# A hybrid decoder layer on one core: k's token rows turned in 32 by 32 blocks by VectorE instead of by TensorE, and a new order of the work before the first FFN products

## What is computed

```
def _mixer_inputs(x, shift, scale, g_pre, w_in, b_f):
    h = _rmsnorm(x, g_pre) * (1.0 + scale) + shift
    q, k, v, f, u, bg, cg, ga, gb = _split_cols(h @ w_in, IN_SIZES)
    logf = jax.nn.log_sigmoid((f + b_f).astype(jnp.float32))
    heads = lambda t: t.reshape(B, T, N_HEADS, HEAD_DIM)
    return heads(q), heads(k), heads(v), logf, cg * u, bg, ga, gb
...
def _finish(x, o, y_conv, bg, ga, gb, gate1, shift2, scale2, gate2, ...):
    m = (jax.nn.sigmoid(ga) * a + jax.nn.sigmoid(gb) * b) @ w_o
    x = x + gate1 * _rmsnorm(m, g_post1)
    h = _rmsnorm(x, g_pre2) * (1.0 + scale2) + shift2
    g, u = jnp.split(h @ w_ffn_in, 2, axis=-1)
    f = (jax.nn.silu(g) * u) @ w_ffn_out
    return x + gate2 * _rmsnorm(f, g_post2)
```

## Time and profile before

| | |
|---|---|
| time, median of 3 runs | 1783.26 us (1783.14 to 1783.98) |
| the profiled execution's own time | 1783.0 us |
| its span | 1781.4 us |
| PE busy | 1768.5 us (99% of the span) |
| DVE busy | 911.0 us (51%) |
| ACT busy | 693.8 us (39%) |
| POOL busy | 26.1 us (1%) |
| data moved | 382.38 MB, 215 GB/s on average |
| granted PE clock | 1.0 of full speed |

### The profile page before, as it was taken

The page is one execution under the profiler, slowest core; times in us unless marked ns, Lnnn a source line. Parts: engine busy times, 40 slices in busy tenths (PEclk is TensorE's granted clock), DMA queues, the critical chain, the costliest instruction groups (busy, mean ns, idle before and its releaser), DMA issues.

```text
span 1781.4 us, 31779 instructions
## 1 busy us (share of the span) xinstructions
PE 1768.5 (99%) x13592; PEld 1664.2 (93%) x13592; DVE 911.0 (51%) x1137; ACT 693.8 (39%) x809; POOL 26.1 (1%) x76
## 2 busy tenths in 40 slices
PE   8999999999999999999999999999999999999999
PEld 6888888897699999998979999999999999999998
DVE  4666663245644344455686444434443445566565
ACT  5332232235643333343354233333333334445454
POOL 0000100001000000000000000000000000000000
PEclk9999999999999999999999999999999999999999
DMA  9988578856754444458866444444444444444441
GB/s 380 409 333 336 214 309 343 355 200 223 262 185 165 163 159 167 162 196 343 332 245 265 142 166 165 165 165 165 165 165 165 165 163 166 164 163 164 163 161 71
DMA packets 59234, 382.38 MB, mean 215 GB/s; under 512 B 6912, under 2 KB 7728, under 8 KB 17026
## 3 DMA queue, kind: packets, MB, share of 16 engines
q1 hardware_dynamic: 57632, 378.27, 56.0%
q0 software_dynamic: 1328, 2.58, 0.4%
q10 hardware_dynamic: 178, 0.13, 0.0%
HBM read 376.15 MB, written 4.81 MB: 214 GB/s over the span
## 4 chain that ended last, share of the span: by engine, by line
PE 96%; DMA 1%; DVE 1%; ACT 1%; issue 1%; SPq 0%; DVEq 0%; ACTq 0%
PE bank L675 29%; PE bank L677 29%; PE bank L676 28%; PE bank L695 3%; PE bank L685 1%; PE bank L972 1%; DMA ada<-in_w_ada 1%; PE bank L1102 1%; PE bank L1071 0%; PE bank L1290 0%; DMA ada_o<-in_w_ada 0%; PE bank L1041 0%; PE bank L951 0%; PE bank L1051 0%; PE bank L898 0%
## 5 line engine op out<-in xcount | busy, mean ns | idle before, releaser
L675 PE MATMUL bank<-a_lo,w_hi 128*128 128x288 f32 x3624 | 1077.0, 297 | 1.4 <-DVE a_lo L1978 0.7
L676 PE MATMUL bank<-a_hi,w_hi 128*128 128x288 f32 x3624 | 1069.1, 295 | 0.0
L677 PE MATMUL bank<-a_hi,w_lo 128*128 128x288 f32 x3624 | 1065.5, 294 | 0.0
L1794 DVE TENSOR_TENSOR w_lo<-raw,w_hi 128x2048 fp32r<-128x2048 f32 x239 | 547.9, 2292 | 699.9 <-ACT w_hi L1327 699.2
L1327 ACT CAST w_hi<-raw 128x2048 fp32r<-128x2048 f32 x238 | 453.9, 1907 | 850.2 <-PE bank L677 824.7
L675 PEld LDWEIGHTS bank<-a_lo,w_hi 128*128 128x128 f32 x3624 | 678.9, 187 | 20.7 <-issue 19.2
L677 PEld LDWEIGHTS bank<-a_hi,w_lo 128*128 128x128 f32 x3624 | 682.6, 188 | 0.0
L676 PEld LDWEIGHTS bank<-a_hi,w_hi 128*128 128x128 f32 x3624 | 680.3, 188 | 0.0
L1906 DVE TENSOR_TENSOR a_lo<-hid,a_hi 128x1152 fp32r<-128x1152 f32 x44 | 59.4, 1351 | 12.3 <-ACT a_hi L1351 12.3
L1351 ACT CAST a_hi<-hid 128x1152 fp32r<-128x1152 f32 x44 | 50.7, 1154 | 0.0
L675 PE MATMUL bank<-o_lo,w_hi 128*128 128x288 f32 x128 | 37.9, 296 | 0.0
(11 more groups left out here) (387 smaller groups left out, 973.4 us busy)
## 6 DMA issues: line engine op xcount, KB each, us to landing
raw<-in_w_ffn_in SPq DMA_DIRECT2D x88, 1024.0 KB, 4.8
raw<-in_w_in SPq DMA_DIRECT2D x75, 1024.0 KB, 7.9
ada<-in_w_ada SPq DMA_DIRECT2D x60, 1024.0 KB, 8.9
raw<-in_w_ffn_out SPq DMA_DIRECT2D x44, 1024.0 KB, 4.8
ada_o<-in_w_ada SPq DMA_DIRECT2D x24, 1024.0 KB, 8.4
raw<-in_w_o SPq DMA_DIRECT2D x16, 1024.0 KB, 4.9
ada<-in_w_ada SPq DMA_DIRECT2D x16, 512.0 KB, 12.6
raw<-in_cache_k SPq DMA_DIRECT2D x16, 512.0 KB, 4.2
```

The costliest lines, as they stand in the source:

```text
L675: pe.matmul(acc, w_hi[buf][:, a, cols], lo[:, kt, :], start=first and a == 0, stop=False)
L676: pe.matmul(acc, w_hi[buf][:, a, cols], hi[:, kt, :], start=False, stop=False)
L677: mm = pe.matmul(acc, w_lo[buf][:, a, cols], hi[:, kt, :], start=False, stop=last and a == tiles - 1)
L1794: tt(w_lo[buf][:, :, :], raw[s][:, :, :], w_hi[buf][:, :, :].bitcast(F32), ALU.subtract).then_inc(raw_turn, 1)
```

## The change

It has two parts that do not touch each other.

1. k is no longer turned by PE. DVE transposes each half of kT in blocks of 32 by 32 (`turn_k_blocks`, one instruction on 128 partitions by 1152 numbers for each half) into a new buffer `k_blocks`. In it a token's channels lie on the partition of the token in pieces of 32, so ACT issues the stores piece by piece (`store_k`): for each half 16 stores for the prompt (32 partitions, 8 blocks, runs of 32 numbers, which is 128 bytes; 32 KB each) and 4 for the samples (16 KB each), 40 in all. The six `turn_rows` and six `copy_row` of k are gone, and so are POOL's two stores of k.
2. Around the first FFN product: the last squares are added on PE by one more matmul and no longer by DVE; the samples of the last w_o tiles are evicted first; two w_ada slots move to another region, so that their loads wait for an earlier product; the w_ada slots are used in another order, 8 of them before the first FFN product, 3 between its halves and 1 inside the second half; and a_hi and a_lo of tiles 0 and 1 are made and waited for one by one (`h2_tiles`).

The core of the diff:

```diff
-    ROWS = ([("k", half, b) for half in range(2) for b in range(3)]
-            + [("v", 0, 0), ("v", 0, 1), ("v", 1, 0), ("v", 1, 1), ("v", 0, 2), ("v", 1, 2)])
+    ROWS = ([("v", 0, 0), ("v", 0, 1), ("v", 1, 0), ("v", 1, 1), ("v", 0, 2), ("v", 1, 2)])
+    K_STORES = 4 * (KA + 2)
...
@@ SP, load_f1 @@
+                    if first and t == 3:
+                        sp.wait_ge(mm_turn, MT * (SPLIT + N_F1 - 2))
+                        for q in range(2, SK):
+                            load_t(q)
                     load_w(N_F1 + PER_F1 * i + t, t % RAW, slot(w_ffn_in, part * F1S + i, k))
                     if first and t == 3:
-                        sp.wait_ge(mm_turn, MT * (SPLIT + N_F1))
-                        for q in range(2, SK):
-                            load_t(q)
-                        for q in range(SK):
-                            sp.wait_ge(ada_turn, RAW + SK * ADA_T + q + 1)
+                        for q, used in enumerate((1, 2, 5, 6)):
+                            sp.wait_ge(ada_turn, RAW + SK * ADA_T + used)
                             sp.dma_start(ada_o[q][:, :, :], slot(w_ada, ADA_T + 2 - SPARE, q)).then_inc(ada_full[q], 16)
...
@@ PE @@
                 if u == 19:
                     sums_of_lf()
-                    pe.wait_ge(ada_turned, 1 + len(ADA_AT))
-                    pe.wait_ge(ada_mods, A_B1 + 1)
-                    pe.wait_ge(bank_turn, BT + MT * (G_QKV + 3))
-                    turn_rows(0)
-                    turn_rows(1)
                 if u == 20:
                     turn_suf()
-                if u == 21:
-                    pe.wait_ge(sufT_done, 1)
-                    pe.wait_ge(bank_turn, BT + MT * (G_QKV + 6))
-                    for n in range(2, 6):
-                        turn_rows(n)
...
-            sum_partitions(MT + LAST, Q_O + KT)
+            sum_partitions(MT + LAST - 1, Q_O + KT)
...
-            ada_rows(0, ada_o, use=ADA_T + 1 - SPARE, last=False, parts=(1, 2, 3))
-            ada_rows(1, ada_t, ada_t_full, first=False, last=False)
-            ada_rows(2, ada_o, use=ADA_T + 2 - SPARE, first=False, last=False, parts=(0, 1))
+            ada_rows(0, ada_o, use=ADA_T + 1 - SPARE, first=False, last=False, parts=(1,))
+            ada_rows(1, ada_t, ada_t_full, first=False, last=False, parts=(3, 2))
+            ada_rows(0, ada_o, use=ADA_T + 1 - SPARE, first=False, last=False, parts=(2, 3))
+            ada_rows(1, ada_t, ada_t_full, first=False, last=False, parts=(0, 1))
...
@@ ACT @@
+            def store_k(half):
+
+                tiles = slice(KA // 2 * half, KA // 2 * half + KA // 2)
+                prompt = k_prompt[0, 0].rearrange("(j r) (k x) (y c) -> x y r k j c", r=32, x=2, y=2)
+                sample = k_sample[0].rearrange("s t (k x) (y c) -> x y (s t) k c", x=2, y=2)
+                act.wait_ge(k_turned, half + 1)
+                for i in range(4):
+                    rows = slice(32 * i, 32 * i + 32)
+                    for k in range(KA // 2 * half, KA // 2 * half + KA // 2):
+                        act.dma_start(prompt[i // 2, i % 2, :, k, :, :],
+                                      k_blocks[rows, k, 0:TP].rearrange("p (j c) -> p j c", c=32)).then_inc(s_kout, 16)
+                    act.dma_start(sample[i // 2, i % 2, :, tiles, :], k_blocks[rows, tiles, TP:NT]).then_inc(s_kout, 16)
...
                     ins.then_inc(sufT_done, 1)
+                    store_k(0)
                 if u == 22:
-                    copy_row(act, nc.scalar.copy, 2)
-                    copy_row(act, nc.scalar.copy, 4)
+                    store_k(1)
...
@@ DVE @@
                 if u == 20:
                     copy_sums()
-                    copy_row(dve, nc.vector.tensor_copy, 1)
-                if u == 22:
-                    copy_row(dve, nc.vector.tensor_copy, 3)
-                    copy_row(dve, nc.vector.tensor_copy, 5)
+                    turn_k_blocks(0)
+                if u == 21:
+                    turn_k_blocks(1)
...
-            h2_times_rstd(0)
+            h2_tiles()
             x1_add(1, x1_times(1))
-            h2_lo(0)
             x1_samples(1)
             h2_times_rstd(1)
```

More of the change, by code:

```diff
@@ L325, in layer @@
         ada_t = [place(f"ada_t{s}", [P, SK, SN], where=o_qkv + 2 * B_ACT8 + s * SK * SN * 4) for s in range(2)]
-        ada_t += [place(f"ada_t{2 + j}", [P, SK, SN], where=off_act + j * KT * NT * 4 + 2 * SK * NT * 4) for j in range(2)]
+        ada_t += [place(f"ada_t{2 + j}", [P, SK, SN], where=off_act + j * KT * NT * 4) for j in range(2)]
         assert SK * SN * 4 <= 2 * SK * NT * 4
@@ L951, in turn_rows @@
                     mm = pe.transpose(bank[ROW_BANK[n]][0:rows, j * P:j * P + P],
-                                      (kT if name == "k" else vT)[:, 4 * half + j, b * P:b * P + rows], ident[:, :])
+                                      vT[:, 4 * half + j, b * P:b * P + rows], ident[:, :])
                 mm.then_inc(rowT_ps, 1)
@@ L1205, in sum_partitions @@
                 pe.matmul(bank[7][:, 0:NT], ones[:, 0:P], sqr[:, :], start=True, stop=False)
+                pe.wait_ge(sq_done, last - 1)
+                pe.matmul(bank[7][:, 0:NT], ones[:, 0:P], sq4[:, MT - 2, :], start=False, stop=False)
                 pe.wait_ge(sq_done, last)
                 pe.matmul(bank[7][:, 0:NT], ones[:, 0:P], sq4[:, MT - 1, :], start=False, stop=True).then_inc(ms_ps, 1)
-            sum_partitions(MT + LAST, Q_O + KT)
+            sum_partitions(MT + LAST - 1, Q_O + KT)
             evicted = BT + MT * (G_O + O_ADA + 1)
@@ L1241, in first_f1 @@
                     if h == 0:
+                        pe.wait_ge(h2_hi, 1)
+                        pe.wait_ge(h2_s, 1)
+                        for mt in range(MT):
+                            pe.wait_ge(bank_turn, BT + MT * G_F1 + mt + 1)
+                            acc, cols = bank[mt][:, 0:NT], slice(mt * P, mt * P + P)
+                            pe.matmul(acc, w_hi[0][:, 0, cols], a_hi[:, 0, :], start=True, stop=False)
+                            pe.matmul(acc, w_lo[0][:, 0, cols], a_hi[:, 0, :], start=False, stop=False)
+                        pe.wait_ge(h2_lo_first, 1)
+                        for mt in range(MT):
+                            pe.matmul(bank[mt][:, 0:NT], w_hi[0][:, 0, mt * P:mt * P + P], a_lo[:, 0, :], start=False,
+                                      stop=False)
                         pe.wait_ge(h2_first, 1)
                     else:
-                        ada_rows(2, ada_o, use=ADA_T + 2 - SPARE, first=False, parts=(2, 3))
+                        ada_rows(2, ada_o, use=ADA_T + 2 - SPARE, first=False, last=False, parts=(0, 1, 2))
                         pe.wait_ge(act_lo, 10 + 1)
                     for mt in range(MT):
-                        if h == 0:
-                            pe.wait_ge(bank_turn, BT + MT * G_F1 + mt + 1)
+                        if h == 1 and mt == 2:
+                            ada_rows(2, ada_o, use=ADA_T + 2 - SPARE, first=False, parts=(3,))
                         acc, cols = bank[mt][:, 0:NT], slice(mt * P, mt * P + P)
-                        for a in (PIECE * h, PIECE * h + 1):
-                            pe.matmul(acc, w_hi[0][:, a, cols], a_lo[:, a, :], start=a == 0, stop=False)
+                        for a in (1,) if h == 0 else (PIECE, PIECE + 1):
+                            pe.matmul(acc, w_hi[0][:, a, cols], a_lo[:, a, :], start=False, stop=False)
                             pe.matmul(acc, w_hi[0][:, a, cols], a_hi[:, a, :], start=False, stop=False)
@@ L1517, in _ @@
                     evict(u, 1)
-                    copy_row(act, nc.scalar.copy, 6)
+                    copy_row(act, nc.scalar.copy, 0)
                     evict(u, 2)
@@ L1662, in gated @@
                     kt = bass.ds(MT * i + mt, 1)
+                    samples = dst[:, kt, TP:NT].rearrange("p a n -> p (a n)")
+                    if last is not None:
+                        nc.scalar.copy(samples, bank[mt][:, TP:NT]).then_inc(s_done, 1)
                     nc.scalar.activation(sq4[:, mt, :], bank[mt][:, 0:NT], ACT.Square).then_inc(sq_done, 1)
-                    nc.scalar.activation(dst[:, kt, 0:TP].rearrange("p a n -> p (a n)"), bank[mt][:, 0:TP],
-                                         ACT.Identity, scale=modG[:, kt, 0:1].rearrange("p a n -> p (a n)"))
-                    ins = nc.scalar.copy(dst[:, kt, TP:NT].rearrange("p a n -> p (a n)"), bank[mt][:, TP:NT])
+                    ins = nc.scalar.activation(dst[:, kt, 0:TP].rearrange("p a n -> p (a n)"), bank[mt][:, 0:TP],
+                                               ACT.Identity, scale=modG[:, kt, 0:1].rearrange("p a n -> p (a n)"))
                     if last is None:
-                        ins.then_inc(bank_turn, 1)
+                        nc.scalar.copy(samples, bank[mt][:, TP:NT]).then_inc(bank_turn, 1)
                         continue
@@ L2198, in copy_KT, with turn_k_blocks @@
```

(5 more changed lines are left out.)

97 lines of the change are left out of this document (54 added, 43 removed).

## The result

The changed kernel takes 1786.43 us (median of 22 runs, 1785.35 to 1788.20), the kernel before 1783.16 beside it. The ratio is 1.0018 with a 95% interval of 1.0012 to 1.0023: 3.3 us longer, at most 4.1. I had forecast 1782.9, a gain of 0.4. The time lies inside the range, the sign is wrong.

The account below looks back on a forecast made before the run. PE was taken to bound the kernel (96% of the chain). Part 1, -2.6 + 2.5 = -0.1 us, and part 2, -0.3, sum to -0.4 from 1783.26, rounded to 1782.9 us; range 1780.0 to 1789.0.

Parts of the forecast that it names:

- Part 1, what comes on ACT: 40 DMA issues in ACT's list, ahead of product 23's cast and copy_KT(0, 0), lose PE 2.5 us.
- I take 0.43 us for each: Each ACT store issue was priced at 0.43 us, ends 0.36 and 0.56, so 20 take 8.6 us.
- the issues take longer: Rival: ACT needs over 0.5 us per store; slower by over 0.2% from 0.53; 1788.1 at 0.56; chance 0.28 including slow draining.
- further than 0.5 us apart: Sign that the forecast is wrong: ACT's store issues stand more than 0.5 us from each other.
- The formula: PE's loss from ACT's issues: 40 p - 14.7 us, not below 0, p the distance of two issues; 2.5 at 0.43.
- The start of the issues: ACT's issues begin when the fourth copy of bias_s is handed over, taken as 0.8 us (0 to 1.5), at 389.5.
- The two waits: PE waits about 1.2 us before product 23 and another 1.3 us before its third column tile.
- 2.6 us leave PE: 24 transposes of k at 0.109 us leave PE's list, 0.87 us before product 20 and 1.75 before product 22.
- forecast 386.6: Before product 21, turn_suf starts on PE at about 386.6, where it started at 387.46, after DVE's sums.
- DVE's transposes: Two transposes of 1152 columns on DVE take 1.4 us each, covered by its gaps, so they cost nothing.
- The runs of 128 bytes: 9216 store runs take 3 to 160 us of the 16 engines; they hold ACT up only above 30 ns each.
- Part 2 was sized at -0.3: Around the first FFN product: 0.3 us gained, between -1.2 and +0.5, the rest becoming a wait for DVE.

Follow-up runs that it names:

- e1: Only the hunks of k (k's rows by DVE, stores issued by ACT), against the kernel before: 1787.21 us, ratio 1.0024.
- e5: The changed kernel with only store_k(0) issued; the second half of k's output is not written: 1784.68 us, ratio 1.0008 to the kernel before.
- e7: The changed kernel with the 32 prompt stores written as contiguous 1 KB for each partition: 1784.47 us, ratio 1.0009 to the kernel before.
- e9: e5 with 16 idle PE transposes of the identity in front of product 23: 1783.23 us, ratio 1.0002 to the kernel before.
- e10: The changed kernel, all 40 stores by ACT, with 16 idle PE transposes in front of product 23: 1787.83 us, ratio 1.0028 to the kernel before.
- e3: The changed kernel with the same 40 stores issued by SP between its loads of cache pages: 1780.26 us, ratio 0.9985 to the kernel before.
- e4: The changed kernel with the 40 stores issued by POOL: 1780.22 us, ratio 0.9984 to the kernel before.
- e6: The changed kernel with only store_k(1) issued; the first half of k's output is not written: 1781.47 us, ratio 0.9990 to the kernel before.

## Why the prediction was wrong

**The step that failed** is the cost of the issues in "Part 1, what comes on ACT": "I take 0.43 us for each". The size was wrong, not the mechanism. Measured were 0.554 us, so 40 of them take 22.2 us and not 17.2. It was the rival "the issues take longer" that came true, at 0.554 past its point of decision of 0.53, and the sign "further than 0.5 us apart" showed it. The formula's other numbers held but for the start of the issues. With that corrected as below, 40 x 0.554 - 15.5 - 2.6 is +4.1 us for part 1, where the traces show +3.97 and e1 alone +4.1. Three things make up the difference of 0.12 us, or 5.0 us over 40 issues. An undisturbed issue of this form is 0.50 apart from the next (2.49 us from one five to the next, above): 2.7 us. One early issue takes 1.52 us, and one of 1.2 us stands there in e1, e5, e7, e9 and e10 too: 1.0 us. And four groups of four take 2.1 to 2.5 us where 1.96 is usual: 1.3 us. These four lie where SP's page loads run (DMA share of 0.6 to 1.1 in the windows, 0.3 to 0.4 at the undisturbed ones). That the loads stretch them is likely but was not tried by itself. e7 bears out the form as a part; the cause of the long single issue stays open. I had the earlier trace rows before me, with distances of 0.43 and 0.56 us and issues from 0.36 to 0.53, and took a value near the low end for a transfer of more dimensions than any in them.

**The start of the issues.** "I take 0.8 us (between 0 and 1.5)" was 0: they ran beside the copies of bias_s. This was 0.8 us in the change's favour. By luck it offset a part of the error in the issues.

**The two waits** stood where they were foretold, ahead of product 23 and ahead of its third column tile, with 3.1 and 1.5 us instead of 1.2 and 1.3.

**The clock** was missing among the terms and the rivals. In the profiled execution of the changed kernel it cost nothing, since bank 4 came free only at 413.2, and PE would have waited 3.1 us there instead of 1.5. The 22 executions agree: six have a mean granted clock of 1.000 and a median of 1786.5 us, the other sixteen one of 1786.4. In e5 it cost 1.4 us.

**What was right.** 2.6 us leave PE; e3 and e4 show them together with part 2's 0.3 as 2.9 each. turn_suf at 388.08 - 1.47 = 386.61 (forecast 386.6). DVE's transposes 1.38 and 1.37 us (1.4), hidden in its gaps. The stores land in 1.9 us and `pair_hi(0)` does not wait. The runs of 128 bytes were bounded by 3 to 160 us with all 16 engines at work; 10034 packets at 11 ns are 110 us of one engine, or 7 us of all 16. The Trainium skill, DMA: Bandwidth & Descriptors, section Specifications, has transfers below 512 bytes run under line rate. The estimate worked out from that ahead was at least 22 ns for each run; the trace has half of that, and the measurement decides. Part 2 was sized at -0.3 and measures -0.34 in both traces: no wait for a reload, the FFN's start at 919.81 - 5.44 = 914.4 (914.5), the transpose's end at 931.01 - 5.44 = 925.6 (924.9 to 925.6), and the gain left over turned into a wait for DVE, of 0.4 us where I had 0.8.

**A better version** is e4 or e3: the change as it is, the stores by POOL or SP. Both are 2.9 us under before, with intervals that exclude no change.

## What to carry to other kernels

A DMA issue is work of the engine that issues it: count the issues, price each at the longest near row, and ask whether the next compute instruction in that list is one that the bounding engine waits for. If it is, give the issues to an engine with nothing urgent behind them, even one that needs longer for each. And when a change makes TensorE wait for a few microseconds in one piece, reckon on 1 to 2 us more behind the wait (1.4 between e5 and e9, 1.6 by the trace), unless a later wait takes them in.

## What the runs showed of the hardware

- Around product 23, TensorE's granted clock fell to 0.50 for 3 to 4 us after standstills of 1.9 (e7), 2.5 (e5), 2.7 (e1) and 3.1 us (changed kernel), and stayed 1.00 after 0.8 (e9), 1.0 (e6) and 1.5 us (the changed kernel's second wait).
- Length alone does not decide. After 2.7 us in e10 the clock stayed at 1.00 in the profiled execution; by the mean clock it fell somewhere in six of nine. Near the kernel's start it fell after waits of only 0.54, 1.22 and 0.49 us within 6 us (changed kernel), and stayed 1.00 after 0.54, 1.12 and 0.49 in e9. What else decides was not tried.
- An issue of 32 partitions by 8 runs of 128 bytes takes 0.49 to 0.50 us on SP and ACT when undisturbed, 0.47 with 1 KB in one piece, and 0.57 on POOL.
- ACT's DMA issues overlap both casts and copies of its own: the first stood at 390.07 beside a copy begun at 390.06.
- A transpose of 128 x 1152 fp32 in SBUF, in blocks of 32, takes 1.38 us on DVE, 1.9 times that of 512 columns out of PSUM.
